# Sums of squares over partitions from a high and a low part, each a single-pass product

## What is computed

```python
def _rmsnorm(x, gain):
    xf = x.astype(jnp.float32)
    y = xf * lax.rsqrt(jnp.mean(xf * xf, axis=-1, keepdims=True) + RMS_EPS)
    return (y * gain.astype(jnp.float32)).astype(x.dtype)
...
    # recurrence: per head, over its 128 channels
    o = _rmsnorm(o, out_norm) * jax.nn.silu(heads(g.astype(jnp.float32)))
...
    # latent attention: per head, over its 128 + 64 channels
    q = _rope_tail(_rmsnorm(q, q_norm), cos, sin)
    k = _rope_tail(_rmsnorm(k, k_norm), cos, sin)
```

## Time and profile before

| | |
|---|---|
| median of 3 runs | 2090.29 us (2089.08 to 2091.22) |
| profiled execution: its time, its span | 2093.21 us, 2091.4 us |
| TensorE busy (matmuls) | 2038.1 us, 97% |
| VectorE, ScalarE, GpSimd busy | 916.7, 909.6, 847.8 us |
| the recurrence's heads | from about 861 to 1130 us |
| the latent heads | from about 1556 to 1694 us |

### The profile page before, as it was taken

The page is one execution under the profiler, slowest core; times in us unless marked ns, Lnnn a source line. Parts: engine busy times, 40 slices in busy tenths (PEclk is TensorE's granted clock), DMA queues, the critical chain, the costliest instruction groups (busy, mean ns, idle before and its releaser), DMA issues.

```text
span 2091.4 us, 23319 instructions
## 1 busy us (share of the span) xinstructions
PE 2038.1 (97%) x9356; PEld 1659.9 (79%) x9356; DVE 916.7 (44%) x1436; ACT 909.6 (43%) x1254; POOL 847.8 (41%) x672
## 2 busy tenths in 40 slices
PE   7999999989999998999999999999999999999999
PEld 6777787768888886788887888888877778888887
DVE  5622223334310323877886355055154544531551
ACT  6455444244323323555555444234256644432441
POOL 1243333435444454233334354444432234444542
PEclk9999999999999999999999999999999999999999
DMA  6122222223333332112121233333310222332332
GB/s 240 51 80 71 81 68 74 81 81 91 101 100 88 104 94 88 41 61 71 52 70 61 81 111 101 101 91 101 100 44 26 84 71 81 111 99 83 106 96 71
DMA packets 51659, 178.09 MB, mean 85 GB/s; under 512 B 5728, under 2 KB 8928, under 8 KB 51424
## 3 DMA queue, kind: packets, MB, share of 16 engines
q1 hardware_dynamic: 51552, 176.61, 27.2%
HBM read 174.49 MB, written 2.10 MB: 84 GB/s over the span
## 4 chain that ended last, share of the span: by engine, by line
PE 93%; DVE 4%; ACT 2%; POOL 1%; issue 1%; DMA 0%; SPq 0%; ACTq 0%
PE ps_gemm L225 24%; PE ps_gemm L227 24%; PE ps_gemm L226 24%; PE ps_attend L225 3%; PE ps_attend L227 3%; PE ps_attend L226 3%; PE ps_attend L1415 2%; PE ps_attend L755 1%; PE ps_attend L2195 1%; PE ps_attend L740 1%; PE ps_attend L766 1%; PE ps_attend L2261 1%; PE ps_attend L2196 1%; PE ps_attend L257 1%; ACT weights_high L200 1%
## 5 line engine op out<-in xcount | busy, mean ns | idle before, releaser
L2454 POOL TENSOR_TENSOR weights_low<-weights_raw,weights_high 128x512 fp32r<-128x512 f32 (+1 forms) x334 | 423.4, 1268 | 1222.1 <-ACT weights_high L200 1221.7
L225 PE MATMUL ps_gemm<-normed_high,weights_high 128*128 128x512 f32 x1672 | 667.4, 399 | 14.5 <-DVE normed_low L286 12.3
L227 PE MATMUL ps_gemm<-normed_low,weights_high 128*128 128x512 f32 x1672 | 653.5, 391 | 0.0
L226 PE MATMUL ps_gemm<-normed_high,weights_low 128*128 128x512 f32 x1672 | 653.3, 391 | 0.0
L200 ACT ACTIVATE weights_high<-weights_raw 128x1024 fp32r<-128x1024 f32 (+1 forms) x341 | 340.7, 1005 | 440.2 <-PE ps_attend L227 208.4
L2455 POOL TENSOR_TENSOR weights_low<-weights_raw,weights_high 128x512 fp32r<-128x512 f32 (+1 forms) x334 | 440.0, 1317 | 0.0
L225 PEld LDWEIGHTS ps_gemm<-normed_high,weights_high 128*128 128x128 f32 x1672 | 315.7, 189 | 86.1 <-DVE normed_low L286 13.9
L226 PEld LDWEIGHTS ps_gemm<-normed_high,weights_low 128*128 128x128 f32 x1672 | 315.8, 189 | 66.6 <-issue 3.8
L227 PEld LDWEIGHTS ps_gemm<-normed_low,weights_high 128*128 128x128 f32 x1672 | 315.2, 188 | 66.8
L225 PE MATMUL ps_gemm<-operands_high_low,weights_high 128*128 128x512 f32 x576 | 227.6, 395 | 6.1 <-DVE operands_high_low L1002 3.3
L227 PE MATMUL ps_gemm<-operands_high_low,weights_high 128*128 128x512 f32 x576 | 225.4, 391 | 0.0
(11 more groups left out here) (282 smaller groups left out, 2081.7 us busy)
## 6 DMA issues: line engine op xcount, KB each, us to landing
weights_raw<-weights_full SPq DMA_DIRECT2D x317, 512.0 KB, 3.6
weights_raw<-weights_short SPq DMA_DIRECT2D x24, 128.0 KB, 2.1
residual<-x_tiles SPq DMA_DIRECT2D x4, 512.0 KB, 7.5
out_tiles<-residual SPq DMA_DIRECT2D x8, 256.0 KB, 2.1
parameters<-params SPq DMA_DIRECT2D x1, 1559.5 KB, 9.1
scratch<-memory_tiles SPq DMA_DIRECT2D x2, 512.0 KB, 6.9
scratch<-positions SPq DMA_DIRECT2D x1, 256.0 KB, 10.0
parameters<-params SPq DMA_DIRECT2D x1, 136.5 KB, 2.2
```

The source lines that it names most:

```text
L225: t.op.matmul(out, m.wh[:, c:c + P], xh, start=start and n == 0, stop=False, skip_group_check=True)
L226: t.op.matmul(out, m.wl[:, c:c + P], xh, start=False, stop=False, skip_group_check=True)
L227: ins = t.op.matmul(out, m.wh[:, c:c + P], xl, start=False, stop=stop and n == len(pairs) - 1, skip_group_check=True)
L2454: g.op.tensor_tensor(m.wl[:, a], m.raw[:, a], m.wh[:, a].bitcast(F32), ALU.subtract)
```

## The change

The sum's operand is split like a large product's: a high part, rounded to fp32r by a ScalarE copy, and a low part, the remainder, which VectorE subtracts. The matrix of ones is copied to an fp32r tile once in each stage. TensorE then makes two products of fp32r operands into the same PSUM bank instead of one fp32 product. This is done for heads 0 to 6 of the recurrence and for k of all 8 latent heads. The sum of recurrence head 7, the sums of q (L2120), and those of the other norms stay as they are.

```diff
+def pe_split_sum(m, t, event, out, ones, parts):
+
+    for n, x in enumerate(parts):
+        ins = t.op.matmul(out, ones, x, start=n == 0, stop=n == 1, skip_group_check=True)
+    ins.then_inc(*m.T.mark(*event))
...
+def head_squares(m):
+
+    return m.high_tile(16), m.high_tile(17), m.high_tile(18)[:, 0:P]
+
+
 def pe_finish(m, t, i):
-    t.wait_ge(*m.A.at("hgrn", "head_square", i))
+
+    hi, lo, ones = head_squares(m)
     if i:
         t.wait_ge(*m.A.at("hgrn", "cross", i))
-    pe_sum_over_partitions(m, t, ("hgrn", "total", i), m.ab(1), m.ss[:, :])
+    if i == KD - 1:
+        t.wait_ge(*m.A.at("hgrn", "head_square", i))
+        pe_sum_over_partitions(m, t, ("hgrn", "total", i), m.ab(1), m.ss[:, :])
+    else:
+        t.wait_ge(*m.A.at("hgrn", "ones"))
+        t.wait_ge(*m.V.at("hgrn", "square_low", i))
+        pe_split_sum(m, t, ("hgrn", "total", i), m.ab(1), ones, (hi, lo))
...
@@ act_attend
     s.op.activation(x.o, out_bank(m, i), ACT.Copy).then_inc(*m.A.mark("hgrn", "o", i))
+    if i < KD - 1:
+        s.wait_ge(*m.A.at("hgrn", "head_square", i))
+        s.op.activation(head_squares(m)[0], m.ss[:, :], ACT.Copy).then_inc(*m.A.mark("hgrn", "square_high", i))
...
@@ act_recurrence
     act_norm_start(m, s, "hgrn", ("hgrn", "f", 0))
+    s.op.activation(head_squares(m)[2], m.col("ones", 0, P), ACT.Copy).then_inc(*m.A.mark("hgrn", "ones"))
...
+def dve_head_square_low(m, v, i):
+    hi, lo, _ = head_squares(m)
+    v.wait_ge(*m.A.at("hgrn", "square_high", i))
+    if i:
+        v.wait_ge(*m.T.at("hgrn", "total", i - 1))
+    v.op.tensor_tensor(lo, m.ss[:, :], hi.bitcast(F32), ALU.subtract).then_inc(*m.V.mark("hgrn", "square_low", i))
...
@@ dve_head
     dve_keep_level(m, v, i, 0)
+    if i:
+        dve_head_square_low(m, v, i - 1)
     dve_distances(m, v, i, 3)
...
@@ Latent
-        self.ident, self.mask = m.nl[:, 0:P], m.nl[:, P:2 * P]
+        self.ident, self.mask, self.ones = (m.nl[:, n * P:(n + 1) * P] for n in range(3))
+        self.sqk_high, self.sqk_low = m.nh[:, 0:TILE], m.nh[:, TILE:2 * TILE]
...
@@ act_latent
     s.op.activation(x.ident, m.col("ident", 0, P), ACT.Copy)
+    s.op.activation(x.ones, m.col("ones", 0, P), ACT.Copy)
     s.op.activation(x.mask, m.col("mla_mask", 0, P), ACT.Copy).then_inc(*m.A.mark("mla", "matrices"))
...
@@ act_front, at its end
+    s.wait_ge(*m.V.at("mla", "sum_k", h))
+    s.op.activation(x.sqk_high, x.sqk, ACT.Copy).then_inc(*m.A.mark("mla", "sqk_high", h))
...
@@ dve_front, at its end
     if h == 0:
         sum_k()
+    v.wait_ge(*m.A.at("mla", "sqk_high", h))
+    v.op.tensor_tensor(x.sqk_low, x.sqk, x.sqk_high.bitcast(F32), ALU.subtract).then_inc(*m.V.mark("mla", "sqk_low", h))
...
@@ pe_stats
-    t.wait_ge(*m.V.at("mla", "sum_k", h))
+    t.wait_ge(*m.V.at("mla", "sqk_low", h))
     t.wait_ge(*(m.A.at("mla", "rstd_k", h - 1) if h else m.A.at("mla", "key_rope")))
-    pe_sum_over_partitions(m, t, ("mla", "total_k", h), m.gb(3), x.sqk)
+    pe_split_sum(m, t, ("mla", "total_k", h), m.gb(3), x.ones, (x.sqk_high, x.sqk_low))
     t.wait_ge(*m.V.at("mla", "sum_q", h))
```

## The result

The changed kernel takes 2109.64 us (median of 6 runs, 2108.52 to 2111.20) against 2091.49 for the kernel before beside it (6 runs, 2089.08 to 2092.51): ratio 1.0089 [1.0079, 1.0099]. It is 18 us slower; +8.2 was forecast, and 2109.6 lies outside the range. The profiled execution has a span of 2109.4 us (2091.4 before) and a mean granted clock of 0.985 (0.992 before).

A forecast was written before the change was run, and what follows sets the result against it. The prediction took the kernel as bound by TensorE's own stream. Recurrence -1.6 us and latent stage +9.8 us summed to +8.2 us, giving 2098.5 us against a median of 2090.29, range 2094 to 2102.5.

The forecast's parts named there:

- +1.61: Latent heads 2 to 6: scores start 1.61 us later per head, waiting for the low part, product saving counted.
- +1.6: Latent head 7: scores start 1.6 us later, with bounds 1.0 to 2.1.
- Rival 1: Latent stage: other work covers the low part, only the product saving is seen, 2085.5 us; chance 0.04.
- rival 2: Latent stage: the wait is real but partly given back, about +3 us, so 2093; chance 0.09.
- rival 4: Both stages: a pair of products isn't cheaper, 0.86 us each, 19 us more, 2117; chance 0.01.
- 0.6 of VectorE's delay: Recurrence, last head: the low part ahead of VectorE's contended multiplications costs about 0.6 us, bounds 0 and 1.8.
- The 0.2 for the copy of the ones: Recurrence start: copying the ones on ScalarE ahead of the first sigmoid costs 0.2 us.
- rival 3: TensorE's clock falls after the new gaps; six falls cost some 9 us more, 2108; chance 0.04.
- The upper bound of the recurrence's part: Recurrence as a whole: forecast -1.6 us, at worst +0.3 us.

The follow-up runs named there:

- the kernel with the gap filled: Kernel before with only the latent edits, plus six unused TensorE products ahead of the low-part wait in heads 2 to 7: 2099.21 us, ratio 1.0036.
- the late old product: Kernel before with only the latent copies, subtractions and waits, the one fp32 product kept but made once the low part is ready: 2111.15 us, ratio 1.0092.

## Why the prediction was wrong

**Right: the direction, the new bound and its price.** The pair waits for VectorE's subtraction in head 0 and in heads 2 to 7, six times for about 1.7 us, as forecast. The period without a fall is 15.44 us against 13.89, +1.55 where the sum had +1.61. The start of the eight small products stands +0.55 us later at head 0 (forecast +0.55), then +0.07 at head 1 (forecast +0.15), +1.65 at head 2 (forecast 1.76). With the clock at 1.00 throughout, the stretch is 9.0 us longer against 9.8. The terms of this part held to a tenth of a microsecond or so each, but for head 7: its scores start 15.44 us after the previous head's in the kernel with the gap filled, 14.17 before, so +1.3 where the sum had +1.6. Rival 1, that the cover holds, is refuted by the waits; rival 2, that later waits give something back, by the even periods; rival 4 by the pair's 0.45 us at head 1, where it doesn't wait.

**Right: the recurrence up to its last wait.** The head sums start 33.47 us apart instead of 33.88, -0.41 for each head. In the last head the across products start 0.19 us later after the last head sum than before: 0.6 of VectorE's delay less 0.41 saved, as forecast. The 0.2 for the copy of the ones isn't there: the stretch with it takes 49.50 us instead of 49.47.

**Wrong: the clock.** In the sum, a fall of the clock behind the new waits stands at nothing. The step that failed is the one on rival 3 by which it was left out: "The trace speaks against it, with new gaps of under 2 us between 12 us of full work." That gave it 0.04. The clock fell behind four of the six waits of 1.7 us (heads 2, 3, 5 and 7) in the profiled execution, and cost 1.7, 3.4, 3.4 and about 3.3 us: 11.7 in all. The rival had priced six falls at 1.5 each, so it had the number of falls too high and the price of one too low (it took the price from a window that ended before the clock came back), and that its 2108 is 1.6 us from the measurement is partly luck: the two errors partly cancel. The same fall came behind the last head's wait in the recurrence: from the across products to the last head's sum it takes 20.45 us instead of 18.95, +1.5, which eats most of the -1.8 saved before. The forecast had nothing for this.

The inference was weak because it rests on two places of one profile. I set one where the clock stayed up against one where it fell and took their difference for a rule. The third line of the earlier trace rows covers the wait itself; behind it the profile before has

```profile
...
1110.90:1113.00 2.10, 2.08 (x15) 2.01 (x16) 2.10 (x6) 2.07 (x3) 0.00 (x0) 1.00 0.00 0
...
```

The other profiles show how far that carries:

- This wait of the last head was followed by 1.00 in all six profiles whose recurrence is as before, without filling there. It was followed by a fall in both with six heads, where it is 2.6 us as well, and in all three with seven, where it is 3.6.
- The wait of 2.6 us in head 0 (888 us) was followed by a fall in all eleven profiles that don't fill it.
- The wait of 1.8 us behind the latent stage, in code that no edit touches, was followed by a fall in four of the thirteen profiles.

So the length of a wait alone doesn't tell whether the clock falls behind it, and neither does the code around it. The rule of the Trainium skill that I had set beside it (TensorE: Matmul & The Clock Gate, A second HAM failure mode), on short idling between groups of matmuls, described this case better than my reading of one row, and the trace after agrees: granted clock 0.90 over 120 us of the stage (1580 to 1700), where it was 1.00.

Two slips have no part in the miss. The upper bound of the recurrence's part, +0.3, doesn't come out of its terms (-2.4 + 1.8 + 0.2 is -0.4). And `sum_k` was 2.5 us old when the sum started, not three (it ends at 1603.42).

**Shown and not shown.** That the clock's fall behind the waits carries 12 of the 20 us is shown by filling: added work made the kernel faster, the clock was 1.00 and all periods were equal. That the wait and not the kind of product brings the fall is shown by the late old product. What decides whether a given wait is followed by a fall stays open: the same latent stage has falls behind different heads in two kernels, waits of 1.0 us had both outcomes, and so had those of 1.8 and of 2.6 us. Each kernel has one profile, so whether its falls move from one execution to the next isn't shown (the mean granted clock of the changed kernel's six executions lies between 0.985 and 0.987).

## What to carry to other kernels

Where TensorE is the chain, ask of each shortened product which input it needs next and when: here 0.40 us was to be gained per head, and a subtraction queued behind a rotation made it a loss of 1.55. Price a new wait of TensorE at its length plus a clock fall of 1.7 to 3.4 us behind it in half of the cases or more (here four of six waits of 1.7 us in each of three profiles, and three of six waits of 1.0 us), and put the likeliest number there instead of the wait alone. Where a wait can't be removed, unused products ahead of it are worth a try.

## What the runs showed that was not expected

- TensorE's granted clock can fall to 0.50 (1.2 GHz) behind waits of 1.7 us, and of 1.0 us, in an otherwise full stream; a fall cost 1.7 or 3.4 us here, and the rest of the period was untouched.
- Six unused products of 0.23 us in each of six such gaps made the kernel 12 us faster; ten in each of two gaps of the kernel before, with the single-pass sums of six heads, gave 4.0 us below the kernel before.
- The same latent stage had its falls behind heads 2, 3, 5 and 7 in one kernel and behind 2, 5, 6 and 7 in another, and a wait that all thirteen kernels share was followed by a fall in four of their profiles.
